# Expert stage: TensorE's side work in small pieces over the slots, one head's later projection per unit, the other tokens' squares summed on VectorE

## The reference, cut to what matters

```
x = x + gate1 * (o @ w_o)                       # output product
h2 = rmsnorm(x) * g * (1 + scale2) + shift2
qp = h2 @ w_pq                                  # 8 heads x 256: "projection"
sc = qp . sub_keys                              # 2 x 128 scores a head
s1, s2 = top 16 of each half; cand = s1 + s2; 16 best of 256; gate = softmax
for each token, head and chosen expert e (16 a head):
    a = h2 . peer_u[e];  w = gate * gelu(a);  y += w * peer_v[e]
x = x + gate2 * y
```

## Time and profile before

| | us |
|---|---|
| median of three runs | 2890.35 (2888.9 to 2893.51) |
| profiled execution, its own time | 2895.25 |
| its span, first to last instruction | 2892.9 |
| first slot's dot of units 0, 1, 2, 3, 4 | 1540.9, 1582.8, 1628.4, 1678.1, 1734.6 |
| first slot's dot of units 5 to 10 | 1775.0, 1817.5, 1860.4, 1904.2, 1949.0, 1990.9 |

### The profile page before, as it was taken

How to read it: one execution, slowest core, us unless ns; L and a number is a source line. 1 busy time by engine, 2 the same in 40 slices (tenths; PEclk the granted TensorE clock), 3 DMA queues, 4 the chain that set the end, 5 groups by cost and what they waited for, 6 DMA issues and landing times. The chain is left out here.

```text
span 2892.9 us, 36754 instructions
## 1 busy us (share of the span) xinstructions
PE 2448.4 (85%) x12516; PEld 1714.6 (59%) x12516; DVE 2091.7 (72%) x4032; ACT 995.8 (34%) x2030; POOL 1161.9 (40%) x961
## 2 busy tenths in 40 slices
PE   7998979999999999999998988887666767666666
PEld 6998979999999896455565534333222222222222
DVE  7466866777777887455547767778877888788876
ACT  3222246666666622343332222222222222221221
POOL 3453346666666530111003334344444434434442
PEclk9999989999999999999999989998898888888888
DMA  3232832222221066011019989999999999999998
GB/s 114 83 98 76 247 95 59 59 58 58 58 58 54 20 199 194 22 30 30 8 45 363 363 352 400 415 390 420 421 420 416 398 422 421 416 393 421 421 421 332
DMA packets 266302, 670.63 MB, mean 232 GB/s; under 512 B 13605, under 2 KB 197066, under 8 KB 200378
## 3 DMA queue, kind: packets, MB, share of 16 engines
q0 software_dynamic: 73952, 536.91, 45.2%
q1 hardware_dynamic: 191616, 131.83, 15.3%
q10 hardware_dynamic: 602, 0.24, 0.0%
HBM read 666.83 MB, written 2.10 MB: 231 GB/s over the span
## 5 line engine op out<-in xcount | busy, mean ns | idle before, releaser
L2614 PE MATMUL peer_py<-peer_uv,peer_diag 128*128 128x512 f32 x1536 | 840.4, 695 | 323.2 <-ACT peer_diag L2473 306.1
L2166 POOL DMA_INDIRECT peer_uv<-k_peer_uv,peer_idx x512 | 510.1, 996 | 794.3 <-PE peer_py L2614 748.8
L2614 PEld LDWEIGHTS peer_py<-peer_uv,peer_diag 128*128 128x128 f32 x1536 | 322.7, 221 | 787.9 <-issue 771.6
L2278 DVE SCALAR_TENSOR_TENSOR peer_spare<-peer_uv,peer_hp 128x1024 bf16<-128x1024 f32 x512 | 622.1, 1217 | 224.6 <-DMA peer_uv<-k_peer_uv,peer_idx 223.7
L1265 PE MATMUL hgrn_pp<-p_hx,p_whl 128*128 128x264 f32 x3024 | 394.4, 289 | 0.8 <-POOL p_whl L1118 0.8
L1265 PEld LDWEIGHTS hgrn_pp<-p_hx,p_whl 128*128 128x128 f32 x3024 | 377.4, 190 | 1.7 <-POOL p_whl L1118 1.2
L2465 ACT ACTIVATE peer_ga<-peer_a 128x2 f32<-128x2 f32 x256 | 52.0, 203 | 815.2 <-DVE peer_spare L2278 815.1
L1118 POOL TENSOR_TENSOR p_whl<-p2n_w,p_whl 128x1024 fp32r<-128x1024 f32 x62 | 147.8, 2394 | 205.7 <-ACT p_whl L1163 205.7
L772 PE MATMUL pool_ps<-p_raw,pool_wh 128*128 128x264 f32 x1024 | 171.9, 291 | 15.6 <-POOL pool_wl L899 10.3
L2473 ACT ACTIVATE peer_diag<-keep_ident,peer_wt 128x128 f32<-128x128 f32 x384 | 140.2, 396 | 127.8 <-DVE peer_wt L2287 123.2
L899 POOL TENSOR_TENSOR pool_wl<-pool_w,pool_wh 128x1024 fp32r<-128x1024 f32 (+1 forms) x48 | 102.9, 2147 | 155.5 <-ACT pool_wh L839 155.5
(11 more groups left out here) (440 smaller groups left out, 4253.7 us busy)
## 6 DMA issues: line engine op xcount, KB each, us to landing
p2n_w<-in_hgrn_w_in SPq DMA_DIRECT2D x62, 512.0 KB
pool_w<-in_pool_w_in SPq DMA_DIRECT2D x32, 512.0 KB, 4.1
pool_out_aw<-in_w_ada SPq DMA_DIRECT2D x16, 768.0 KB, 4.6
hgrn_out_aw<-in_w_ada SPq DMA_DIRECT2D x16, 768.0 KB, 4.7
p_w<-in_w_pq SPq DMA_DIRECT2D x12, 1024.0 KB, 8.4
peer_uv<-k_peer_uv,peer_idx POOLq DMA_INDIRECT x512
pool_out_w<-in_pool_w_out SPq DMA_DIRECT2D x7, 1024.0 KB, 7.5
p3a_wf<-in_w_in SPq DMA_DIRECT2D x12, 512.0 KB, 6.5
```

The costliest lines, as they stand in the source:

```text
L2166: pool.indirect_dma_start(out=uv[:, n % DEPTH].rearrange("p w d -> p (w d)"), out_offset=None, in_=io["k_peer_uv"], in_offset=bass.Indirec ...
L2278: dve.scalar_tensor_tensor(out=spare[:, n % 2, :], in0=uv[:, n % DEPTH, 0, :], scalar=1.0, in1=hp[:, t % 2, :], op0=ALU.mult, op1=ALU.mult ...
L2614: last = pe.matmul(py[:, h * 512:(h + 1) * 512], diag[:, products(n) % DIAGS, :], uv[:, n % DEPTH, 1, h * 512:(h + 1) * 512], start=n % (P ...
```

## The change

- Projections are cut into pieces of one or more matmuls (`begin`, `end`). An early one (heads 3, 4, 5 for the first tokens) is spread over slots 0 to 7 of units 0, 1 and 2, head 2's is done ahead of the loop.
- The later ones are in a new order, `LATE`: 6, 7, 0, 1, 2, 3, 4, 5, one head in each of units 3 to 10: its first half in slots 0 to 4, its second in slots 6 to 10 (`PIECES`).
- Head 4's weights for the other tokens are loaded again (13 loads instead of 12). `frees` lets a load off by the same head's last piece, as before.
- The other tokens' output products are placed one after even slots and two after odd ones in both of units 0 and 1, with new places in `EVACS`.
- TensorE's `column` is left for the first tokens only. For the others VectorE adds each block's squares into `keep["total"]` (`add_square`, places in `ADDS`), ScalarE's next square waits for it, and TensorE sums once (`columns`, three matmuls). `root` reads the sums from PSUM.
- The root, the scaling and the shift in unit 2 stand one to three slots later, as do the transposes of units 5 and 6.

```diff
@@ peer_phase @@
-        loads = [(0, 0), (1, 1), (2, 0), (3, 1), (4, 0), (5, 1), (6, 0), (7, 0), (0, 0), (1, 0), (2, 0), (3, 0)]
-        frees = {2: (0, None, FIRST), 3: (1, None, FIRST), 4: (2, None, FIRST), 5: (3, None, FIRST), 6: (4, 1, REST),
-                 7: (6, 1, WHOLE), 8: (7, 1, WHOLE), 9: (0, 1, REST), 10: (1, 1, REST), 11: (2, 1, REST)}
...
+        LATE = ((6, WHOLE), (7, WHOLE), (0, REST), (1, REST), (2, REST), (3, REST), (4, REST), (5, REST))
...
+        loads = [(0, 0), (1, 1), (2, 0), (3, 1), (4, 0), (5, 1), (6, 0), (7, 0), (0, 0), (1, 0), (2, 0), (3, 0), (4, 0)]
+        frees = {i + 2: (i, None, FIRST) for i in range(5)}
+        frees.update({i + 7: (n, 1, span) for i, (n, span) in enumerate(LATE[:6])})
+        PIECES = {0: (0, 2), 1: (2, 4), 2: (4, 5), 3: (5, 7), 4: (7, 8)}
+        EVACS = {(0, 9): 2, (0, 14): 3, (1, 3): 4, (1, 9): 5, (1, 14): 6, (2, 3): 7}
+        ADDS = {(0, 1): 1, (0, 12): 2, (1, 1): 3, (1, 6): 4, (1, 12): 5, (2, 1): 6, (2, 5): 7}
...
+            def add_square(m):
+
+                dve.wait_ge(sq_done, KC + m + 1)
+                to = keep["total"][:, 0:SEQ - P]
+                if m == 0:
+                    dve.tensor_copy(to, sq[:, :]).then_inc(sq_added, 1)
+                else:
+                    dve.wait_ge(sq_added, m)
+                    dve.tensor_tensor(to, to, sq[:, :], ALU.add).then_inc(sq_added, 1)
...
+            take_q(2, None, FIRST)
...
+                    if s < 3 and at == 4:
+                        take_q(3 + s, None, FIRST)
+                    if 3 <= s < 3 + PH and at in (3, 6):
+                        take_q(LATE[s - 3][0], 0 if at == 3 else 1, LATE[s - 3][1])
...
+            def columns():
+
+                pe.wait_ge(sq_added, KC)
+                for j in range(TT - 1):
+                    last = pe.matmul(pair[0][:, SEQ - P + j:SEQ - P + j + 1], keep["total"][:, j * P:(j + 1) * P],
+                                     keep["ones"][:, 0:1], start=True, stop=True)
+                last.then_inc(n_summed, 1)
...
+            project(2, None, FIRST)
             for s in range(UNITS):
...
-                    if (s, k) in WITHIN:
-                        project(*WITHIN[s, k])
+                    if s < 3 and k < PH:
+                        project(3 + s, None, FIRST, 2 * k, 2 * k + 2)
+                    if 3 <= s < 3 + PH and k % 6 in PIECES and k < 11:
+                        n, span = LATE[s - 3]
+                        project(n, k // 6, span, *PIECES[k % 6])
...
                     if s < 2:
-                        fill(1 + s)
-                    if s == 2 and k == 3:
-                        column(KC - 1, REST)
+                        fill(1 + k % 2)
+                    if s == 2 and k == 5:
+                        columns()
```

More of the change, by code:

```diff
@@ L2120, in weights_in @@
         def weights_in(n, span):
-            last = max(i for i, (h, b) in enumerate(loads) if h == n and (i < PH or span == REST and n < 4))
+            last = max(i for i, (h, b) in enumerate(loads) if h == n and (i < PH or span == REST and n < 5))
             b = loads[last][1]
@@ L2323, in take_out, with add_columns @@
                                          in1=x, op0=ALU.mult, op1=ALU.add).then_inc(o_taken, 1)
[L2325 to L2335, removed]
+            def add_columns():
+                dve.wait_ge(n_summed, 1)
+                dve.tensor_reduce(roots[:, 0:1], pQ[:, 0:KC], AX_X, ALU.add).then_inc(added, 1)
+            def add_square(m):
[6 more added lines that the diff above has]
+                    dve.tensor_tensor(to, to, sq[:, :], ALU.add).then_inc(sq_added, 1)
             def invert(span):
@@ L2429, in square @@
                 act.wait_ge(o_taken, m + 1 + (KC if span == REST else 0))
+                if span == REST and m:
+                    act.wait_ge(sq_added, m)
                 act.activation(sq[:, 0:b - a], xT[:, m, a:b], ACT.Square).then_inc(sq_done, 1)
             def root(span):
[L2433 to L2435 removed]
+                if span == FIRST:
+                    act.wait_ge(added, 1)
+                    to = at = roots[:, 0:1]
+                else:
+                    act.wait_ge(n_summed, 2)
+                    to, at = roots[:, 1:TT], pair[0][:, SEQ - P:SEQ - P + TT - 1]
+                act.activation(to, at, ACT.Sqrt, bias=keep["eps"][:, 0:1], scale=1.0 / D).then_inc(rooted, 1)
             def shift(c, span):
@@ L2481, in _ @@
                             square(m, REST)
-                    if s == 2 and at == 2:
+                    if s == 2 and at == 3:
                         root(REST)
-                    if s == 2 and at >= 5:
-                        for c in {5: (0, 1), 6: (2, 3, 4, 5), 7: (6, 7)}[at]:
+                    if s == 2 and at >= 6:
+                        for c in range(6) if at == 6 else (6, 7):
                             shift(c, REST)
-                    if s == 5 and at == 6:
+                    if s == 5 and at == 7:
                         act.wait_ge(x_turned, 1)
                         act.activation(g2, hp[:, 1, :], ACT.Copy).then_inc(x_taken, 1)
-                    if s == 6 and at == 0:
+                    if s == 6 and at == 2:
                         take_x(0)
@@ L2518, in out_products, with column @@
                     last.then_inc(o_summed, 1)
[L2520 to L2526, removed]
+            def column(m):
+                pe.wait_ge(sq_done, m + 1)
+                last = pe.matmul(pQ[:, m:m + 1], sq[:, 0:P], keep["ones"][:, 0:1], start=True, stop=True)
                 if m == KC - 1:
                     last.then_inc(n_summed, 1)
+            def columns():
[4 more added lines that the diff above has]
+                last.then_inc(n_summed, 1)
             def spread_roots(span):
@@ L2542, in fill, with project @@
                     m, k = divmod(i, KC)
-                    if k == KC - 1 and m:
-                        column(m - 1, REST)
                     out_products(m, k, REST)
                 placed[0] += n
-            def project(n, j, span):
+            def project(n, j, span, begin=0, end=None):
                 i = part_at[n, j, span]
                 a, b = span
-                if j is None or j == 0:
-                    slot, times = weights_in(n, span)
+                slot, times = weights_in(n, span)
+                end = end or (2 * KC if j is None else KC)
+                if begin == 0 and j != 1:
                     pe.wait_ge(w_in[slot], times * 16)
-                slot = weights_in(n, span)[0]
-                if i:
+                if begin == 0 and i:
                     pe.wait_ge(q_taken, i)
-                for half in range(2) if j is None else (j,):
+                for x in range(begin, end):
+                    half, c = divmod(x, KC) if j is None else (j, x)
                     to = pQ[:, half * P:(half + 1) * P] if j is None else pQ[:, a:b]
[L2559 to L2566, removed]
+                    if i == 0 and half == 0:
+                        pe.wait_ge(ready, c + 1)
+                    if (n, j, span) == (6, 0, WHOLE):
+                        pe.wait_ge(ready, KC + c + 1)
+                    last = pe.matmul(to, w[:, slot, c, half * P:(half + 1) * P], h2[:, c, a:b],
+                                     start=c == 0, stop=c == KC - 1)
+                if end == (2 * KC if j is None else KC):
+                    last.then_inc(projected, 1)
             def scores(r):
@@ L2586, in _ @@
                     if k == KC - 1 and m:
-                        column(m - 1, FIRST)
+                        column(m - 1)
                     out_products(m, k, FIRST)
             fill(1)
-            column(KC - 1, FIRST)
+            column(KC - 1)
             fill(1)
```

44 lines of the change are left out of this document (16 added, 28 removed).

## The result

The changed kernel takes **2926.85 us** (median of 4 runs, 2923.58 to 2930.97) against 2891.93 for the kernel before beside it: ratio 1.0122, 95% interval 1.0104 to 1.0139, slower by 35 us. The forecast was 2912, slower by 0.7%.

The account below looks back on a forecast made before the run. Expert-row gathers over DMA were taken as the expert stage's limit, with TensorE holding them up in early units. Terms -23.5 + 2.5 + 42.5 = +21.5 us on 2890.35 gave 2912 us, range 2882 to 2930.

Parts of the forecast that it names:

- rival three: Expert stage: the stall spreads through late gelus, or VectorE's additions and full TensorE eat the early gain; 2930 us, chance 0.12.
- the early gain: Units 0 to 4: lost DMA time won back by spreading side work, 23.5 us, with 15 to 26 allowed.
- Lost DMA time: Expert stage: (421 - rate) x length / 421 per unit; 33 us to be had in all.
- Part one: Units 0 to 3: side work spread out takes back all but 3 of 26.5 us lost, -23.5 us.
- VectorE's cost of nothing: Units 0 to 2: VectorE's added copy and additions, 3 to 4.5 us, are covered by the gathers.
- Part two: Head 4's weights are read again: 1.05 MB, +2.5 us of DMA time.
- Part three: Units 4 to 9: 25 us weight loads get only six slots, 16 to 17 us, so TensorE waits; +42.5 us.
- Rival one: Later projections: the load lands within its six slots, so the kernel gets faster, 2868 us; chance 0.15.
- The whole-packet rule: Weight loads: an engine drains about 9 to 17 descriptors from one queue before turning; estimate 14 to 24 us a load.
- Rival two: Units 4 to 9: the stall stops gathers, loads shorten to 20.5 us, loss and gain meet; 2891 us, chance 0.10.
- What would show it: Signs: units 1 to 3 at 40 to 44 us, units 5 to 9 at 48 to 52, weight waits 70 to 95.
- a margin of 2.5 us: Kernel before, later projections: a load took 25 us and TensorE used it after 27.5.

Follow-up runs that it names:

- number 2: The changed kernel with later loads alternating between two weight slots and head 5 loaded a second time (14 loads): 2873.8 us, ratio 0.9950.
- number 7: The kernel with two alternating weight slots, the other tokens' squares summed on TensorE as before, without VectorE's additions: 2875.1 us, ratio 0.9941.
- number 1: The changed kernel with each later projection in two whole halves after slots 2 and 6 instead of pieces: 2871.3 us, ratio 0.9946.
- number 4: The changed kernel with projection weights laid out so a head's 8 KB per partition are contiguous (big packets): 2869.0 us, ratio 0.9936.
- number 6: The kernel with two alternating weight slots, each load cut into two of 128 columns (512-byte packets): 2878.5 us, ratio 0.9968.
- number 5: The changed kernel with later projections' pieces in slots 0 to 6, so the load is let off at slot 6: 2890.4 us, ratio 1.0010.
- number 8: The kernel before with only the projection weights laid out anew, 8 KB contiguous per partition: 2876.5 us, ratio 0.9958.

## Why the prediction was right in kind and short in size

- **The number.** The measured 2926.85 us lies in the range (2882 to 2930), but 15 us above the forecast of 2912 and 2 above the band of 2900 to 2925 that had 0.63. It is near rival three's 2930 without being rival three: gelu waits did not grow, and the early gain was short by 2 us only.
- **Bound and measure.** Lost DMA time was the right yardstick. Its balance gives +37 us against 37 in the traces. (The first sum has a slip: 0.9, 5.7, 4.6, 11.5 and 3.6 add up to 26.3, not 26.5.)
- **Part one, -23.5 us.** Units 0 to 3 alone lose 5.1 us, where I left 3 for units 0 to 4. Against 26.4 before, unit 4's 3.6 included, that is a gain of 21.3, short by 2. The wait of 16.86 us for head 6's weights is gone, as said. Unit 3 has 3.5 of the 5.1: TensorE was busy 37.0 us there for my 34.9, and the rate 385 GB/s. The same instructions ran at 417 GB/s in number 2, so why unit 3 lost here stays open. VectorE's cost of nothing held; number 7 shows that moving the sums off TensorE, some 4 us of its work, brought nothing either, so the gain is that of the spread, of the moved work and of the earlier load.
- **Part two, +2.5 us.** Not refuted; numbers 1 and 2 differ by one load and by 2.5 us, inside their scatter.
- **Part three, +42.5 us: the mechanism was right, the term too small.** Units 4 to 9 lost 62.3 us where I had 49, and less the 6.5 of before that is +55.8 where I had +42.5: 13.3 us are missing, for two reasons. First, the six cycles took 316.3 us, not 310.5: 56.1, 51.6, 52.3, 52.6, 52.3 and 51.5. TensorE's share was good (26.4 for 26.7), the load was not: I let it shrink to 24 us in a drained ring, and it took 25.9, 25.1, 25.1, 25.1, 24.2 and 25.8. Second, I let the DMA deliver 99 slots in that stretch; it delivered some 95 to 96 (99.9 MB). Sixteen slots a unit make 96; the 3 more were gathers that I took to be still under way at the first issue, which the prediction doesn't spell out. TensorE with 16 projection matmuls between its products was behind the gathers instead: at 1699 slot 15 of unit 3 had just landed. Three slots are 7.5 us. The 13.3 us and the 2 of part one are the 15 us of difference.
- **Rival one** did not come: loads land within six slots only in packets of 8 KB (number 4). The whole-packet rule (the Trainium skill, DMA: Bandwidth & Descriptors, Queues, rings and completion order) would have loads of 1 KB rows done in fewer turns than there are rows; numbers 4 and 6 show about one row per turn. **Rival two** is hardly seen in the changed kernel, where one load of six fell to 24.2 us, and real in number 5. **Rival three** did not come: VectorE's longest wait for a gelu was 8.2 us, and all such waits 37.8 us against 41.5.
- **What would show it.** Waits for weights 71.7 us in six (70 to 95 forecast): 13.5, 11.9, 13.0, 13.8, 5.0 and 14.5, where part three had 8 in the first and 16 in the others; units 5 to 9 at 51.5 to 52.5 us (48 to 52) and 331 to 350 GB/s (330 to 370); the first matmuls after a wait at a granted clock of 0.50; GpSimd's waits longer. Unit 1 came as forecast. Unit 3 had the length but 385 GB/s for over 400. Unit 2, at 46.6 us, is over its 44 and over the 45 at which I would have called the early part wrong. That sign was badly chosen: the unit moved 419 GB/s, and I had not thought of gathers getting ahead. The rate should have been the sign, not the length.

## What to carry to other kernels

When side work is spread thinly, check what the last piece lets off and what the first piece needs: here the spread took twelve slots of slack down to six, and a load with a margin of 2.5 us became a wait in each of units 4 to 9. A single-buffered operand makes a loop of load and use; add its two halves up and compare the sum with the period of the engine that should be the limit. The length of a load beside a saturated queue went with its number of packets rather than its bytes, so a layout with long rows can be worth more than another order of instructions: it alone took 12 us off the kernel before (number 8).

## What the runs showed of the hardware that I had not expected

- Two queues on the same DMA engines alternate about row by row, at each of three row sizes, where the prediction had it for one: 1 MB beside 8 KB gathers took some 9, 25 and 44 us in rows of 8 KB, 1 KB and 512 bytes.
- Small rows also cost a little of the rate of all DMA together: in units 5 and 6 it was 420 and 421 GB/s with 8 KB loads, 415 and 416 with 1 KB, 410 with 512 bytes (numbers 4, 2 and 6).
- TensorE at 42.60 of 42.60 us busy in one unit still fed the DMA engines at 417 GB/s; full was not yet too late (number 7).
